# Cross-attention scores and values of a one-core transformer layer: two-pass fp32 products replaced by three fp32r passes over high and low parts

## What is computed

```python
def cross_attention(hn, memn, wq, wkv, wo):          # X_HEADS = 4, X_HD = 256, N_MEM = 256
    q = (hn @ wq).reshape(B, S, X_HEADS, X_HD)
    k, v = jnp.split(memn @ wkv, 2, axis=-1)         # each (B, 256, 4, 256) after the reshape
    logits = jnp.einsum('bqhd,bkhd->bhqk', q, k) * (X_HD ** -0.5)
    p = jax.nn.softmax(logits, axis=-1)
    o = jnp.einsum('bhqk,bkhd->bqhd', p, v).reshape(B, S, D_MODEL)
    return o @ wo
...
h = h + cross_attention(rms_norm(h, norm_xattn), rms_norm(mem, norm_mem), w_xq, w_xkv, w_xo)
```

## Time and profile before

| | |
|---|---|
| median of three runs | 932.28 us |
| profiled execution | 931.21 us; its span 929.2 us, so 2.0 us lie around the span |
| TensorE busy | 914.5 us of the span |
| VectorE busy | 571.6 us |
| ScalarE busy | 437.6 us |
| granted TensorE clock, mean | 0.997 |
| score products (L1687) | 64 records of 32 calls |
| value products (L1736) | 32 records of 16 calls |

### The profile page before, as it was taken

The page is one execution under the profiler, slowest core; times in us unless marked ns, Lnnn a source line. Parts: engine busy times, 40 slices in busy tenths (PEclk is TensorE's granted clock), DMA queues, the critical chain, the costliest instruction groups (busy, mean ns, idle before and its releaser), DMA issues.

```text
span 929.2 us, 11938 instructions
## 1 busy us (share of the span) xinstructions
PE 914.5 (98%) x4578; PEld 752.6 (81%) x4578; DVE 571.6 (62%) x1028; ACT 437.6 (47%) x762; POOL 21.6 (2%) x44
## 2 busy tenths in 40 slices
PE   8999999999999999999999999999999999999996
PEld 6878778777787888889888778988888888888885
DVE  6534677424557645777233545668847966884797
ACT  6544566533533314335243543366346445644654
POOL 5000000000000000000000000000000000000002
PEclk9999999999999999999999999999999999999998
DMA  7411222112201552343521432130432262043202
GB/s 276 137 47 47 87 92 81 41 61 91 91 1 46 184 179 91 113 136 122 174 91 45 136 136 91 46 136 2 150 122 91 72 200 91 1 140 132 91 1 92
DMA packets 44689, 92.11 MB, mean 99 GB/s; under 512 B 1764, under 2 KB 1864, under 8 KB 44632
## 3 DMA queue, kind: packets, MB, share of 16 engines
q1 hardware_dynamic: 43048, 86.02, 27.4%
q0 software_dynamic: 1568, 5.32, 1.8%
q10 hardware_dynamic: 16, 0.00, 0.0%
HBM read 89.24 MB, written 2.10 MB: 98 GB/s over the span
## 4 chain that ended last, share of the span: by engine, by line
PE 86%; DVE 8%; ACT 4%; issue 1%; DMA 1%; SPq 0%; ACTq 0%; DVEq 0%
PE bank L1523 60%; PE bank L1562 16%; DVE w_lo L1131 2%; DVE conv_acc L1218 2%; PE bank L1687 1%; PE bank L1736 1%; PE bank L1575 1%; ACT w_hi L825 1%; PE bank L1673 1%; PE bank L1714 1%; PE bank L1701 1%; DVE peak L1392 1%; PE bank L1629 1%; PE bank L1656 1%; DMA stage<-in_w_in 1%
## 5 line engine op out<-in xcount | busy, mean ns | idle before, releaser
L1523 PE MATMUL bank<-act_hi,w_hi 128*128 128x512 f32 (+1 forms) x640 | 247.8, 387 | 0.1
L1523 PE MATMUL bank<-act_hi,w_lo 128*128 128x512 f32 (+1 forms) x640 | 242.8, 379 | 0.0
L1523 PE MATMUL bank<-act_lo,w_hi 128*128 128x512 f32 (+1 forms) x640 | 242.4, 379 | 0.0
L1127 DVE TENSOR_TENSOR w_lo<-stage,w_hi 128x1024 fp32r<-128x1024 f32 x136 | 162.4, 1237 | 60.7 <-ACT w_hi L825 60.2
L825 ACT ACTIVATE w_hi<-stage 128x1024 fp32r<-128x1024 f32 x136 | 136.3, 1051 | 98.6 <-PE bank L1562 38.2
L1523 PEld LDWEIGHTS bank<-act_hi,w_lo 128*128 128x128 f32 x640 | 120.4, 188 | 23.2
L1523 PEld LDWEIGHTS bank<-act_hi,w_hi 128*128 128x128 f32 x640 | 120.6, 188 | 22.2 <-DVE w_lo L1127 0.6
L1523 PEld LDWEIGHTS bank<-act_lo,w_hi 128*128 128x128 f32 x640 | 120.6, 188 | 21.2
L1523 PE MATMUL bank<-w_hi,act_hi 128*128 128x512 f32 x192 | 76.5, 399 | 2.8 <-DVE act_lo L1346 2.4
L1131 DVE SCALAR_TENSOR_TENSOR w_lo<-stage,gain_col,w_hi 128x512 fp32r<-128x512 f32 x88 | 60.2, 748 | 24.7 <-ACT w_hi L825 24.7
L1523 PE MATMUL bank<-w_hi,act_lo 128*128 128x512 f32 x192 | 74.9, 390 | 0.0
(11 more groups left out here) (287 smaller groups left out, 1340.6 us busy)
## 6 DMA issues: line engine op xcount, KB each, us to landing
stage<-in_w_in SPq DMA_DIRECT2D x20, 1024.0 KB, 5.0
stage<-in_w_mlp_in SPq DMA_DIRECT2D x16, 1024.0 KB, 5.3
stage<-in_w_mlp_out SPq DMA_DIRECT2D x16, 1024.0 KB, 5.5
stage<-in_w_xkv SPq DMA_DIRECT2D x8, 1024.0 KB, 4.9
stage<-in_w_mix_out SPq DMA_DIRECT2D x4, 1024.0 KB, 5.0
stage<-in_w_xq SPq DMA_DIRECT2D x4, 1024.0 KB, 5.9
stage<-in_w_xo SPq DMA_DIRECT2D x4, 1024.0 KB, 5.0
x_tok<-in_x SPq DMA_DIRECT2D x4, 512.0 KB, 7.4
```

The costliest lines, as they stand in the source:

```text
L1127: dve.tensor_tensor(w_lo[:, r:r + 2, :], stage_pair(pair), w_hi[:, r:r + 2, :].bitcast(F32), ALU.subtract).then_inc(s_low, 1)
L1523: ins = pe.matmul(dst, still[q], moving[q], start=(k == 0 and q == 0), stop=(k == nk - 1 and q == 2))
```

## The change

The keys, queries, values and probabilities become fp32r pairs of high and low parts, and `x_scores` and `x_values` make three fp32r passes per product in place of one fp32 call. ScalarE's instructions stay, and now write fp32r high parts. VectorE gets a low part for each: 8 of 128x256 for the keys, 8 of 128x512 for the queries, 4 of 128x512 for the values, and 16 of 128x256 in the step `turned` for the probabilities. In `take` of these units it is now VectorE's instruction that raises `s_taken`. The transposes wait for `s_pt_low` (the low part of the tile two before) and `x_values` waits for it as well. The probabilities move onto the memory of the queries, `mem_k_lo` lies in stage2, and two waits guard reused memory: the first load into stage2 waits for the last score tile, and the load of the final norm's row waits for the values.

```diff
-        mem_k = at("mem_k", 32, [P, KT, MEM])
+        mem_k, mem_k_lo = at("mem_k", 32, [P, KT, MEM], F32R), at("mem_k_lo", -57, [P, KT, MEM], F32R)
-        mem_v = at("mem_v", 84, [P, MEM // P, DM])
+        mem_v = at("mem_v", 84, [P, MEM // P, DM], F32R)
+        mem_v_lo = [at(f"mem_v_lo{j}", kb, [P, DM], F32R) for j, kb in enumerate((74, 92))]
-        x_q = at("x_q", A1, [P, KT, TOK])
-        x_prob_t = at("x_prob_t", A1 + 16, [P, X_HEADS, MEM // P, TOK])
+        x_q, x_q_lo = at("x_q", A1, [P, KT, TOK], F32R), at("x_q_lo", A1 + 16, [P, KT, TOK], F32R)
+        x_prob_t = at("x_prob_t", A1, [P, X_HEADS, MEM // P, TOK], F32R)
+        x_prob_lo = at("x_prob_lo", A1 + 16, [P, X_HEADS, MEM // P, TOK], F32R)
...
# SyncE, before a load
+                elif buf == 2:
+                    sp.wait_ge(s_score, X0 + N_X)
# GpSimd
             pool.wait_ge(s_scaled, 2 * (2 * NT + 2))
+            pool.wait_ge(s_xv, 2 * X_HEADS)
             load_row(row_b, norm_final, s_row_b)
# ScalarE, take
-                    copy(mem_k[:, 4 * order(n) + j, :], b[:, 0:MEM]).then_inc(free, 1)
+                    copy(mem_k[:, 4 * order(n) + j, :], b[:, 0:MEM]).then_inc(s_khigh, 1)
...
# VectorE, take
+                elif k == "mem_k":
+                    t = 4 * order(n) + j
+                    dve.wait_ge(s_khigh, t + 1)
+                    dve.tensor_tensor(mem_k_lo[:, t, :], b[:, 0:MEM], mem_k[:, t, :].bitcast(F32), ALU.subtract)\
+                       .then_inc(free, 1)
+                elif k == "x_q":
+                    dve.wait_ge(s_xqhigh, t + 1)
+                    dve.scalar_tensor_tensor(x_q_lo[:, t, :], b[:], X_HD ** -0.5, x_q[:, t, :].bitcast(F32),
+                                             ALU.mult, ALU.subtract).then_inc(free, 1)
+                elif k == "mem_v":
+                    dve.wait_ge(s_vhigh, MEM // P * order(n) + j + 1)
+                    dve.tensor_tensor(mem_v_lo[j][:, c], b[:], mem_v[:, j, c].bitcast(F32), ALU.subtract)\
+                       .then_inc(free, 1)
...
# VectorE, turned
+                elif step == "turned" and n >= X0:
+                    dve.wait_ge(s_pt, n + 1)
+                    dve.tensor_tensor(x_prob_lo[:, h, :, tok],
+                                      bank[4 + n % 2][:, 0:MEM].rearrange("p (k t) -> p k t", k=2),
+                                      x_prob_t[:, h, :, tok].bitcast(F32), ALU.subtract).then_inc(s_pt_low, 1)
...
# TensorE, x_scores
-                    ins = pe.matmul(bank[2 + t % 2][:, 0:MEM], x_q[:, 2 * h + d, P * i:P * i + P],
-                                    mem_k[:, 2 * h + d, :], start=(d == 0), stop=(d == 1))
+                    for q, (still, moving) in enumerate(((hi, k_hi), (hi, k_lo), (lo, k_hi))):
+                        ins = pe.matmul(bank[2 + t % 2][:, 0:MEM], still, moving, start=(d == 0 and q == 0),
+                                        stop=(d == 1 and q == 2))
# TensorE, turn
                     pe.wait_ge(s_pt, t - 1)
+                    if t >= X0 + 2:
+                        pe.wait_ge(s_pt_low, t - X0 - 1)
# TensorE, x_values
-                pe.wait_ge(s_pt, X0 + NT * (h + 1))
+                pe.wait_ge(s_pt_low, NT * (h + 1))
-                        ins = pe.matmul(x_bank(h, d)[:], mem_v[:, j, col:col + P], x_prob_t[:, h, j, :],
-                                        start=(j == 0), stop=(j == 1))
+                        for q, (still, moving) in enumerate(((v, p), (v, p_lo), (v_lo, p))):
+                            ins = pe.matmul(x_bank(h, d)[:], still, moving, start=(j == 0 and q == 0),
+                                            stop=(j == 1 and q == 2))
```

More of the change, by code:

```diff
@@ L556, in trunk @@
         s_pturn, s_pt, s_value = sem("s_pturn"), sem("s_pt"), sem("s_value")
+        s_khigh, s_xqhigh = sem("s_khigh"), sem("s_xqhigh")
+        s_pt_low, s_vhigh = sem("s_pt_low"), sem("s_vhigh")
         s_yfh, s_yfl = sem("s_yfh"), sem("s_yfl")
@@ L886, in take @@
                 elif k == "mem_k":
-                    copy(mem_k[:, 4 * order(n) + j, :], b[:, 0:MEM]).then_inc(free, 1)
+                    copy(mem_k[:, 4 * order(n) + j, :], b[:, 0:MEM]).then_inc(s_khigh, 1)
                 elif k == "x_q":
-                    act.activation(x_q[:, 4 * order(n) + j, :], b[:], ACT.Copy, scale=X_HD ** -0.5).then_inc(free, 1)
+                    act.activation(x_q[:, 4 * order(n) + j, :], b[:], ACT.Copy, scale=X_HD ** -0.5).then_inc(s_xqhigh, 1)
                 elif k == "mem_v":
-                    copy(mem_v[:, j, HALF_W * order(n):HALF_W * (order(n) + 1)], b[:]).then_inc(free, 1)
+                    copy(mem_v[:, j, HALF_W * order(n):HALF_W * (order(n) + 1)], b[:]).then_inc(s_vhigh, 1)
                 elif k == "mlp_in":
@@ L1238, in take @@
                        .then_inc(s_merged, 1)
+                elif k == "mem_k":
[4 more added lines that the diff above has]
+                elif k == "x_q":
+                    t = 4 * order(n) + j
+                    dve.wait_ge(s_xqhigh, t + 1)
+                    dve.scalar_tensor_tensor(x_q_lo[:, t, :], b[:], X_HD ** -0.5, x_q[:, t, :].bitcast(F32),
+                                             ALU.mult, ALU.subtract).then_inc(free, 1)
+                elif k == "mem_v":
+                    c = slice(HALF_W * order(n), HALF_W * (order(n) + 1))
+                    dve.wait_ge(s_vhigh, MEM // P * order(n) + j + 1)
+                    dve.tensor_tensor(mem_v_lo[j][:, c], b[:], mem_v[:, j, c].bitcast(F32), ALU.subtract)\
+                       .then_inc(free, 1)
                 elif k in ("mix", "x_out"):
@@ L1425, in _ @@
                                              ml_den[:, h, i:i + 1]).then_inc(s_prob, 1)
+                elif step == "turned" and n >= X0:
+                    t = n - X0
+                    h, tok = t // NT, slice(P * (n % NT), P * (n % NT) + P)
+                    dve.wait_ge(s_pt, n + 1)
+                    dve.tensor_tensor(x_prob_lo[:, h, :, tok],
+                                      bank[4 + n % 2][:, 0:MEM].rearrange("p (k t) -> p k t", k=2),
+                                      x_prob_t[:, h, :, tok].bitcast(F32), ALU.subtract).then_inc(s_pt_low, 1)
                 elif step == "fox_split":
@@ L1686, in x_scores @@
                 for d in range(2):
-                    ins = pe.matmul(bank[2 + t % 2][:, 0:MEM], x_q[:, 2 * h + d, P * i:P * i + P],
-                                    mem_k[:, 2 * h + d, :], start=(d == 0), stop=(d == 1))
+                    hi, lo = (v[:, 2 * h + d, P * i:P * i + P] for v in (x_q, x_q_lo))
+                    k_hi, k_lo = mem_k[:, 2 * h + d, :], mem_k_lo[:, 2 * h + d, :]
+                    for q, (still, moving) in enumerate(((hi, k_hi), (hi, k_lo), (lo, k_hi))):
+                        ins = pe.matmul(bank[2 + t % 2][:, 0:MEM], still, moving, start=(d == 0 and q == 0),
+                                        stop=(d == 1 and q == 2))
                 ins.then_inc(s_score, 1)
@@ L1735, in x_values @@
                     for j in range(MEM // P):
-                        ins = pe.matmul(x_bank(h, d)[:], mem_v[:, j, col:col + P], x_prob_t[:, h, j, :],
-                                        start=(j == 0), stop=(j == 1))
+                        v, v_lo = mem_v[:, j, col:col + P], mem_v_lo[j][:, col:col + P]
+                        p, p_lo = (m[:, h, j, :] for m in (x_prob_t, x_prob_lo))
+                        for q, (still, moving) in enumerate(((v, p), (v, p_lo), (v_lo, p))):
+                            ins = pe.matmul(x_bank(h, d)[:], still, moving, start=(j == 0 and q == 0),
+                                            stop=(j == 1 and q == 2))
                     ins.then_inc(s_xv, 1)
```

## The result

| | before | after |
|---|---|---|
| median | 932.25 us (22 runs, 931.30 to 933.56) | 934.27 us (22 runs, 932.91 to 936.28) |
| ratio, 95% interval | | 1.0023 [1.0017, 1.0029] |
| profiled execution | 931.21 us, span 929.2 us | 933.9 us, span 931.8 us |

The changed kernel is 2.0 us slower. Predicted were 933.0 us and a range of 930.1 to 935.6. The forecast's sum was +0.7; the other 1.2 us have to be explained.

What follows compares the result with a forecast made beforehand. TensorE was taken to bound the kernel: 5.06 us saved, against stalls of 2.46, 0.63, 1.25, 1.38 and 0.10, less 0.04 already waited, gave +0.7 us on the 932.28 median, so 933.0 us; range 930.1 to 935.6.

Steps and rivals of the forecast that it cites:

- The bound: Whole kernel: TensorE, busy 98% of the span, sets the time, so product time saved is won unless something comes late.
- The gain: Score and value products in cross-attention: shorter fp32r passes give TensorE 5.06 us less to do.
- weight loads: 48 more loads on TensorE, costed at nothing; the rival that they show: 939 us, chance 0.04.
- key group 70: Key stage: its bank comes free only after VectorE's low part, queued behind weight pairs; TensorE stalls 2.46 us.
- tile 17: Score tiles: low parts of group 79 and tile 16 delay VectorE's scaling; TensorE stalls 0.63 us.
- tiles 24, 25: Score tiles: low parts of group 83 and tile 23 delay the maximum of tile 24; stall 1.25 us.
- tiles 28 to 30: Score tiles: low parts of group 84 and tiles 26, 27, 28 delay VectorE's scaling of tile 30; stall 1.38 us.
- The fifth stall: Values of head 1: TensorE waits for VectorE's `x_split` 0 before `x_values` 1, 0.10 us.
- The clock: Rival: TensorE's granted clock falls after the new 2.46 us gap, adding 1.5 to 3 us (934.5 to 936); chance 0.09.
- the prediction's own signs of being wrong: No idle time at group 70, passes further apart than 0.12 and 0.229, or granted clock under 1.00 after it.
- VectorE was not in time: Rival that VectorE is in time, so stalls together stay under 3.2 us: about 929.9 us, chance 0.17.
- A low part cost: VectorE's queue: 0.33 or 0.60 us each; rival with full record and a trip (0.52, 0.79): 934.7 us, chance 0.14.

Runs made afterwards that it cites:

- experiment 1: Kernel before with scores and values as three fp32r passes, all on high parts, no low parts made: 926.68 us, ratio 0.9949.
- experiment 4: Changed kernel with the takes of key groups 68 and 72 moved ahead of weight pairs 64, 65 and 68, 69: 929.99 us, ratio 0.9988.
- experiment 7: Changed kernel with low parts of probabilities and groups 79, 83, 84 moved into VectorE's wait for ScalarE's exponential; key wait stays: 931.03 us, ratio 0.9996.
- experiment 3: Changed kernel with ten fp32 identity products into an unused bank ahead of key group 70, the wait itself staying: 932.12 us, ratio 1.0005.
- experiment 6: Changed kernel with the take of key group 68 between weight pairs 64 and 65 instead of behind both: 931.31 us, ratio 1.0001.

## Why the prediction came out as it did

**The bound: right.** TensorE's time was won where its products shrank, and lost only where VectorE came late. 62% of VectorE's time was busy before and 63% after; neither number would have shown a wait.

**The gain: right.** 5.06 predicted, 4.86 measured by experiment 1. For **weight loads** I took nothing. Starts of 0.12 us against loads of 0.19 had said so the earlier trace rows, and the experiment agrees. The rule of the Trainium skill, "TensorE: Matmul & The Clock Gate", Part 3, "The mechanism", has loads overlap a matmul only across row groups; load and pass would then stand one behind the other, and by the prediction's estimate no gain would have been left. The trace and experiment 1 disagree with it.

**The waits: right, each within 0.15 us**, counted as the bracket and the 0.15 us by which the key group's delay of 2.42 is more than its 2.27.

| wait | predicted | measured |
|---|---|---|
| key group 70 | 2.46 | 2.42 |
| tile 17 | 0.63 | 0.46 + 0.15 = 0.61 |
| tiles 24, 25 | 1.25 | 1.07 + 0.15 = 1.22 |
| tiles 28 to 30 | 1.38 | 1.08 + 0.15 = 1.23 |

Experiments 4 and 7 show that these are the causes and not only companions: take each away by order alone, and 3.6 and 3.1 us come back (with the clock's part in the first). The fifth stall, 0.10 before the values of head 1, is too small for a row of the waits; that head's twelve passes take 2.86 us in the chain, head 0's 2.74. The sum, +0.7, fits the runs in which the clock held (+0.87), and experiment 3, where it was kept up by dummy work (+0.6). Part of this is chance: the stalls together were predicted 0.2 us too long and the gain 0.2 us too large, and the two cancel.

**The clock: the step that failed.** I had it as a rival with 0.09 and the words "It decides if the gap is a little longer than I think." The gap was as long as I thought, and the clock fell in most runs. Two of the prediction's own signs of being wrong came with it: passes 0.22 us apart, and a granted clock of 0.50. The price was at the lower end of what I gave or under it: +1.5 to +3, where the traces show 1.6, the groups of experiment 7 are 1.3 apart and the first two rows of the table 0.9. The "3 to 6 us" at the lower clock stood on no row; the trace shows 3.4. What was mis-sized above all is the chance. I held the new gap of 2.46 against the one fall that I had, 2.5 us after the last work, took 2.46 for shorter than 2.5, and so for safe. Two numbers that close called for an even chance. Nor is that 2.5 a fixed time: in the other nine traces the fall comes 2.7 to 5.2 us after the last work (the longest in experiment 4, from 919.98 to about 925.2), so the row that I had was the shortest of ten. And in the changed kernel's profile the clock fell at about 433.6, when work had been back for 0.6 us: that work is back does not rule out a fall. The warning in the Trainium skill, "TensorE: Matmul & The Clock Gate", "HAM oscillation", that idle time between bursts throttles the clock, held here for five of six waits of 2.2 to 2.4 us in the traces; experiment 7's profile shows the sixth, without a fall.

So the range held the time, and the sum had the right sign. What had the best chance was missed by a little: 0.62 stood on "within 0.2%" and 0.21 on slower, with the result 2.02 us up where the bound is 1.86, a distance of 0.16 us that the interval is too wide to resolve.

**The other rivals.** VectorE was not in time at any of the four places. A low part cost 0.33 and 0.60 in a queue, not 0.42 and 0.1 each. The new waits on SyncE and GpSimd left no cost that shows: among TensorE's waits none is for a DMA.

**What stays open.** What separates the executions in which the clock falls behind the wait of 2.4 us from those in which it does not; which of the runs without a trace had their fall at the key stage and which at the start, in experiments 6 and 7 above all; and why the early wait is longer in some executions.

## What to carry to other kernels

When an engine with spare time gets small new tasks, ask of each where it stands in that engine's queue and which wait of the critical engine it now ends; a task that frees a buffer belongs ahead of long work, one whose result is wanted late belongs in the engine's own waiting time. Here that order alone was worth 6 us (+2.8 to -3.5 on one chip), more than the whole gain of the faster products. A wait of TensorE like the 2.4 us here should be costed twice, as idle time and as half clock on the work behind it, with at least an even chance for the second where another row shows a fall after about as much idle time.

## What the runs showed of the hardware

- The granted clock can fall after the work is back: idle until 432.97, full clock until about 433.6, then half speed to about 437.0, at a cost of 1.6 us against a trace with the same wait and no fall.
- Of six waits of 2.2 to 2.4 us in the ten traces, five had a fall behind them; of the waits up to 1.7 us none had, among them the one of 1.1 us in experiment 6. By their mean clocks (0.998 and 0.996) executions of one program differ in this.
- Behind the last matmul the clock fell after 2.5 to 5.2 us. Twenty fp32 records of 128 columns in place of the idle time were enough to keep it in the profile of experiment 3.
- Full-height fp32r passes of 256 columns, each with its own weights, start 0.12 us apart while one load's record lasts 0.19.
